# The forget-gate strips of an HGRN branch as seven block products, their weight sums on GpSimd and their snapshots on ScalarE

## The chip, the cores and the metric

The kernel is one program on one core of a Trainium2 chip. The metric is device time in microseconds (us). Everything is float32.

## The reference

A two-layer block feeds a second block. The part that matters is the HGRN branch of the second block's token mix. From 256 latent tokens (taken in column-major order of a 4 x 64 grid, "permuted") and 256 context tokens it computes, for 8 heads of width 128 and in two directions, forget gates and keys from one projection, and then a chunked scan:

```
seg_c = _split_proj(xc @ w_in + b_in)
seg_l = _split_proj(xl @ w_in + b_in)
...
def _hgrn_gates(f_pre, lb):
    fp = f_pre.astype(jnp.float32)
    logf = jnp.log(lb + (1.0 - lb) * jax.nn.sigmoid(fp))
    k = (1.0 - lb) * jax.nn.sigmoid(-fp)
    return logf, k
...
cf, cb, gc = prep(seg_c)
lf, lbw, gl = prep(tuple(_to_col_major(a) for a in seg_l))
hc, hl = _bidir_scan(_hgrn_scan, cf, cb, lf, lbw, init)
```

`f_pre` is what the change is about: 2 directions x 1024 channels, for 256 latent and 256 context tokens each, from 1024 inputs.

## The kernel before

**Layout.** Channels lie on the 128 partitions, tokens along a row. `U` holds the normalized tokens (8 channel tiles, 256 latents and then 256 contexts), `UP` (the memory of `H1`) the latents permuted. Weights come in strips of 256 columns into four slots `W[0]` to `W[3]`. PSUM is eight banks, each handed over by a semaphore `free[b]`. The whole order of work is written out by hand, engine by engine, with counted semaphores between them.

**The recurrence.** The 8 heads are worked in 4 pairs (`i` = 0 to 3). For each pair TensorE projects the query strip (slot 0), one forget strip for each direction (slots 1 and 2) and the value strip (slot 3), and computes the scan as a tree of products: a diagonal product, then levels 0 to 7 (`levels`), context products (`context`), output (`values`) and a mean of squares for the head's norm (the matmul with `mean_c`, here **omean**). On the other engines, level by level, VectorE (`advance`, `pick`) and ScalarE (`lookup`) prepare the operands of the next level.

**The weave.** So that TensorE does not wait for them, the projections of the next pair are Python generators that yield after each matmul, and `weave(steps, n)` issues the next n of them between the levels. I call such a matmul (128 x 128 weights against 256 tokens) a **step**. In pair i the steps are, in this order: value strip of pair i (32), then query strip (16) and forget strips of pair i+1 (32 each, `steps_f`); for the last pair three gate strips (16 each) stand in place of the query and forget strips. `WEAVE` and `WEAVE_LAST` say how many go where; what is left is issued behind omean. The forget strips of pair 0 stand unwoven ahead of the loop (the **opening**), after the query strip.

**A forget strip before** fills two banks, one for each 128 output channels, and in each the 256 latents and the 256 contexts, 8 steps each. When a bank is done ScalarE reads it twice with a sigmoid (`forget`, into `FF_` and `KK`), VectorE scales both (`gates`), and frees the way to `KSUM` (the sum of the keys), which the next pair's diagonal product waits for (`lev_ready`).

**The end of a pair**, in program order: omean; ScalarE turns it into `RS` (a Ln and an Exp); VectorE normalizes and gates the output (`OT`, `HHT`: in the trace L3230 and L3238); the second direction's gates; KSUM. Elsewhere the kernel already uses seven block products in place of eight (`seven_products`), with weight sums on VectorE or half on GpSimd (L1705, L1707), snapshots of PSUM on ScalarE and `assemble` on VectorE.

```
            def token_sums(tokens, o):

                tt(o[0], tokens(0, 1), tokens(0, 0), ALU.subtract).then_inc(S.order_dve, p.inc(S.order_dve))
                eng.wait_ge(S.order_dve, p.now(S.order_dve))
                tt(o[1], tokens(1, 1), o[0], ALU.subtract).then_inc(S.order_dve, p.inc(S.order_dve))
                eng.wait_ge(S.order_dve, p.now(S.order_dve))
                tt(o[2], tokens(1, 1), tokens(0, 1), ALU.subtract)
                tt(o[3], tokens(1, 0), o[1], ALU.subtract).then_inc(S.tsum, p.inc(S.tsum))
```

## Time and profile before

| | |
|---|---|
| time, median of 3 runs | 2031.46 us (2029.79 to 2031.55) |
| the profiled execution's own time | 2030.01 us |
| its span, first to last instruction | 2028.3 us |
| TensorE busy | 1992.8 us (98%) |
| VectorE busy | 1219.1 us (60%) |
| ScalarE busy | 558.7 us (28%) |
| GpSimd busy | 175.7 us (9%) |
| HBM traffic | 270.38 MB read, 134 GB/s over the span |

The busy share is an average over stages. The page cuts the span into 40 slices of 50.7 us; the recurrence lies in slices 29 to 34. PE is TensorE's matmuls, PEld its weight loads, DVE VectorE, ACT ScalarE, POOL GpSimd. A float32 matmul appears as two records, so 16 records are 8 steps.

### The profile page before, as it was taken

The page shows a single profiled execution, that of the slowest core. Times are in us where ns is not written, and L with a number is a line of the kernel's source. Part 1 is how long each engine was busy: PE and PEld are TensorE (multiplying, and loading weights), DVE is VectorE, ACT ScalarE, POOL GpSimd, SP SyncE. Part 2 cuts the span into 40 slices and gives each one's busy share as a digit, 9 for nine tenths or more (in the row PEclk, how much of TensorE's full clock was granted, in tenths as well). Part 3 has the DMA queues.
Part 4 walks back from the last instruction along what each step waited for, and adds up shares of the span by engine and source line. Part 5 has one row for each costly group of instructions (what it writes and reads, how often), then busy time and mean ns, then how long its engine had stood idle before and what let it go on. Part 6 is the DMA issues. An engine that isn't in the chain of part 4 may idle for free.

```text
span 2028.3 us, 31156 instructions
## 1 busy us (share of the span) xinstructions
PE 1992.8 (98%) x12521; PEld 1782.7 (88%) x12521; DVE 1219.1 (60%) x2492; ACT 558.7 (28%) x1342; POOL 175.7 (9%) x232
## 2 busy tenths in 40 slices
PE   9999999999999999999999999999999999999998
PEld 7867999977789999888888878888889889989998
DVE  5424987571278975899769565333344555766664
ACT  3343332223443323111110023222332323232212
POOL 5110341311013300000000001000000000000000
PEclk9999999999999999999999999999999999999999
DMA  6254445442554542555545445332222224545552
GB/s 193 89 166 136 162 162 172 121 144 71 168 166 146 190 144 83 166 166 166 169 156 164 139 122 169 106 96 85 63 79 67 63 63 136 171 131 179 172 175 79
DMA packets 274873, 273.61 MB, mean 135 GB/s; under 512 B 11022, under 2 KB 272378, under 8 KB 274730
## 3 DMA queue, kind: packets, MB, share of 16 engines
q1 hardware_dynamic: 272920, 267.65, 41.4%
q0 software_dynamic: 1216, 3.32, 0.6%
q8 instruction: 100, 1.64, 0.3%
q10 hardware_dynamic: 594, 0.65, 0.1%
q14 instruction: 43, 0.35, 0.1%
HBM read 270.38 MB, written 1.08 MB: 134 GB/s over the span
## 4 chain that ended last, share of the span: by engine, by line
PE 92%; DVE 4%; ACT 1%; DMA 1%; issue 1%; SPq 0%; DVEq 0%; ACTq 0%
PE bank L790 49%; PE bank L1254 11%; PE bank L777 8%; PE bank L1433 5%; PE bank L919 3%; PE bank L1447 2%; PE bank L978 2%; PE bank L1030 1%; PE bank L1498 1%; PE bank L1419 1%; PE bank L1460 1%; DMA W<-in_ada_w_dram 1%; PE bank L989 1%; PE bank L1171 1%; PE bank L1165 1%
## 5 line engine op out<-in xcount | busy, mean ns | idle before, releaser
L790 PE MATMUL bank<-arena,SQ 128*128 128x136 f32 (+2 forms) x2176 | 341.5, 308 | 2.6 <-ACT arena L1793 2.6
L790 PEld LDWEIGHTS bank<-arena,SQ 128*128 128x128 f32 x2176 | 307.0, 191 | 19.8 <-ACT arena L1793 2.8
L790 PE MATMUL bank<-arena,W 128*128 128x136 f32 (+2 forms) x1824 | 272.6, 301 | 2.7 <-issue 2.1
L790 PEld LDWEIGHTS bank<-arena,W 128*128 128x128 f32 x1824 | 247.6, 191 | 15.4 <-issue 4.1
L1793 ACT ACTIVATE H<-bank 128x128 f32<-128x128 f32 (+1 forms) x260 | 82.3, 317 | 537.0 <-PE bank L790 537.0
L790 PE MATMUL bank<-U,W 128*128 128x136 f32 (+2 forms) x1296 | 194.6, 303 | 0.0
L790 PEld LDWEIGHTS bank<-U,W 128*128 128x128 f32 x1296 | 176.4, 191 | 10.9 <-issue 2.9
L777 PE MATMUL bank<-U,W 128*128 128x272 f32 (+2 forms) x608 | 140.6, 392 | 2.4 <-DVEq L2452 1.2
L777 PEld LDWEIGHTS bank<-U,W 128*128 128x128 f32 (+1 forms) x608 | 111.7, 185 | 29.9 <-issue 3.9
L2845 DVE SCALAR_TENSOR_TENSOR W<-W,CC 128x256 f32<-128x256 f32 x280 | 128.3, 483 | 7.0
L790 PE MATMUL bank<-arena 128*128 128x136 f32 (+1 forms) x1024 | 124.1, 278 | 0.0
L790 PEld LDWEIGHTS bank<-arena 128*128 128x128 f32 x1024 | 120.6, 191 | 0.0
L1254 PE MATMUL bank<-W,U 128*128 128x256 f32 (+1 forms) x512 | 100.5, 355 | 0.0
L790 PE MATMUL bank<-U,SQ 128*128 128x136 f32 (+2 forms) x608 | 98.2, 304 | 0.0
L1254 PEld LDWEIGHTS bank<-W,U 128*128 128x128 f32 x512 | 86.8, 190 | 11.5 <-issue 2.0
L1793 ACT ACTIVATE arena<-bank 128x136 f32<-128x136 f32 x176 | 49.1, 279 | 169.9 <-PE bank L790 169.9
L790 PEld LDWEIGHTS bank<-U,SQ 128*128 128x128 f32 x608 | 85.9, 191 | 4.1
L1254 PE MATMUL bank<-arena 128*128 128x256 f32 (+3 forms) x352 | 66.2, 332 | 0.0
L1705 POOL TENSOR_TENSOR SQ<-W 128x512 f32<-128x512 f32 x32 | 40.7, 1272 | 278.9 <-PE bank L790 278.9
L1254 PEld LDWEIGHTS bank<-arena 128*128 128x128 f32 (+2 forms) x352 | 52.2, 179 | 14.1 <-issue 4.0
L2746 DVE SCALAR_TENSOR_TENSOR arena<-arena,PL 128x270 f32<-128x270 f32 x72 | 62.7, 871 | 2.6
L919 PE MATMUL bank<-arena,W 128*128 128x272 f32 x256 | 60.3, 394 | 1.4 <-ACT arena L1783 1.4
(428 smaller groups left out, 3016.2 us busy)
## 6 DMA issues: line engine op xcount, KB each, us to landing
W<-in_ffn_w_up_dram SPq DMA_DIRECT2D x44, 1024.0 KB, 5.1
W<-in_ffn_w_in_dram SPq DMA_DIRECT2D x44, 1024.0 KB, 5.1
W<-in_ada_w_dram SPq DMA_DIRECT2D x36, 1024.0 KB, 7.4
W<-in_mix_w_in_dram SPq DMA_DIRECT2D x36, 1024.0 KB, 5.4
W<-in_w_in_dram SPq DMA_DIRECT2D x22, 1024.0 KB, 5.3
W<-in_ffn_w_down_dram SPq DMA_DIRECT2D x16, 1408.0 KB, 6.5
W<-in_ffn_w_out_dram SPq DMA_DIRECT2D x16, 1408.0 KB, 6.4
W<-in_w_out_dram SPq DMA_DIRECT2D x8, 1024.0 KB, 8.5
```

Of the source, the lines that this page charges most:

```text
L777: last = mm(bank[b][0:m, 0:n], W[r][:, kk, t * P:t * P + m], rhs(kk), start=kk == 0, stop=kk == k - 1)
L790: last = mm(o, a(k), b[:, k], start=not adds and k == 0, stop=k == kt - 1, skip_group_check=True)
L919: return mm(bank[2 * (r % 2) + t][:, c0:c0 + n], W[r][:, k, t * P:(t + 1) * P], rhs(k), start=k == 0, stop=k == KD - 1, skip_group_check=True)
L978: last = mm(o, U[:, kk, t0:t0 + w], W[r][:, kk, 0:SW], start=kk == 0, stop=kk == KD - 1)
L989: last = mm(bank[b][:, 0:T1], W[r][:, kk, t * P:(t + 1) * P], u1(kk), start=kk == 0, stop=kk == KD - 1)
L1254: last = mm(o, x, y, start=i == 0, stop=i == n - 1 and bias is None, skip_group_check=True)
L1433: last = mm(bank[b][:, c:c + SEQ], W[r][:, k, t * P:(t + 1) * P], src[:, k, c:c + SEQ], start=k == 0, stop=k == KD - 1, skip_group_check=True)
L1447: last = mm(bank[b][:, c:c + SW], tok(k), W[r][:, k, :], start=k == 0, stop=k == KD - 1, skip_group_check=True)
L1705: eng.tensor_tensor(WS[n % 2][:, 0], part(1, 0), part(1, 1), ALU.add).then_inc(S.order_pool, p.inc(S.order_pool))
L1793: act(sn[:, i, :], bank[b][:, c:c + w], ACT.Copy).then_inc(S.snap, p.inc(S.snap))
L2746: stt(CZ[:, i, 2:], Z[:, g % 2, i, 0:T1 - 2], w(0), CZ[:, i, 2:], ALU.mult, ALU.add).then_inc(sem, p.inc(sem))
L2845: ins = stt(o, x, c, o, ALU.mult, ALU.add) if k else ts(o, x, c, None, ALU.mult)
```

## The change

Each forget strip is cut into four blocks of weights (two halves of the inputs by two tiles of the outputs) and four blocks of tokens (two halves of the inputs by the two token groups: permuted latents and contexts). Seven products of 4 steps replace eight. They need four sums of token blocks, once (`token_sums` into `TBR`, on VectorE after the second pair of the memory stage that comes before), and four sums of weight blocks for each strip (GpSimd, into `WSR`: a new loop at the end of its program). The partial results are copied out of PSUM as they stand by ScalarE (`kept`, four copies for each strip into `SNR`) and added up on VectorE (`fold`, three additions), which frees the banks; ScalarE's two sigmoids then read the folded result from SBUF. `WSR` shares its memory with `TBU`, so the latents' token sums for the merge move from before the recurrence to its last pair. The numbers of the weave change (pre 14, ctx 12). Two semaphores of the convolution norm become one (no instruction changes). The diff without these declarations:

```
@@ -51,8 +51,8 @@
-WEAVE = dict(pre=10, diag=6, lev=8, ctx=10, av=10, om=12)
-WEAVE_LAST = dict(pre=8, diag=4, lev=6, ctx=8, av=6, om=6)
+WEAVE = dict(pre=14, diag=6, lev=8, ctx=12, av=10)
+WEAVE_LAST = dict(pre=8, diag=4, lev=6, ctx=8, av=6)
@@ -422,6 +423,9 @@
+        SN_LATE = cut(2, SEQ)
+        TBR = [H2[:, 0:4, SEQ:2 * SEQ], H2[:, 4:8, SEQ:2 * SEQ], cut(4, SEQ), cut(4, SEQ)]
+        SNR = [[W[2 * d][:, SK - 1, :], W[2 * d + 1][:, SK - 1, :], SN_LATE[:, 0, :], SN_LATE[:, 1, :]] for d in range(2)]
@@ -461,6 +465,10 @@
+        def permuted_and_context(h, c):
...
+            return (UP[:, 4 * h:4 * h + 4, 0:SEQ], U[:, 4 * h:4 * h + 4, SEQ:2 * SEQ])[c]
@@ -1422,20 +1430,56 @@
-            def steps_f(r):
+            def steps_f(r, first=False):
...
+                bx = 2 * (r % 2)
+                by = bx + 1
+                near, far = slice(0, SEQ), slice(SEQ, 2 * SEQ)
...
+                def raw(t, h, k):
+                    return W[r][:, 4 * h + k, t * P:(t + 1) * P]
...
+                def add(o, x, y, k, clear, ends=True):
+                    ins = mm(o, x, y, start=clear and k == 0, stop=k == 3, skip_group_check=True)
+                    if ends and k == 3:
+                        ins.then_inc(S.prod, p.inc(S.prod))
+                    return ins
                 eng.wait_ge(S.land[r], p.next(S.land[r], 16))
-                for t in range(2):
-                    b = 2 * (r % 2) + t
-                    take(b)
-                    for c, src in ((0, UP), (SEQ, U)):
-                        for k in range(KD):
-                            last = mm(bank[b][:, c:c + SEQ], W[r][:, k, t * P:(t + 1) * P], src[:, k, c:c + SEQ],
-                                      start=k == 0, stop=k == KD - 1, skip_group_check=True)
-                            if c and k == KD - 1:
-                                sem = S.done[r] if t else S.half[r]
-                                last.then_inc(sem, p.inc(sem))
-                            yield
+                take(bx)
+                for k in range(4):
+                    add(bank[bx][:, near], raw(0, 0, k), permuted_and_context(0, 0)[:, k], k, True)
+                    yield
+                take(by)
+                for k in range(4):
+                    add(bank[by][:, near], raw(0, 1, k), permuted_and_context(1, 0)[:, k], k, True, False)
+                    yield
+                if first:
+                    eng.wait_ge(S.tsum, p.next(S.tsum))
+                eng.wait_ge(S.wsum, p.next(S.wsum))
+                eng.wait_ge(S.snap, p.next(S.snap))
+                for k in range(4):
+                    add(bank[bx][:, far], WSR[0][:, k], TBR[0][:, k], k, False)
+                    yield
+                for k in range(4):
+                    add(bank[by][:, far], raw(1, 1, k), TBR[3][:, k], k, True)
+                    yield
+                eng.wait_ge(S.wsum, p.next(S.wsum))
+                eng.wait_ge(S.snap, p.next(S.snap))
+                for k in range(4):
+                    add(bank[bx][:, near], WSR[1][:, k], TBR[1][:, k], k, False)
+                    yield
+                eng.wait_ge(S.wsum, p.next(S.wsum))
+                eng.wait_ge(S.snap, p.next(S.snap, 2))
+                for k in range(4):
+                    add(bank[bx][:, far], WSR[3][:, k], permuted_and_context(1, 1)[:, k], k, False)
+                    yield
+                eng.wait_ge(S.wsum, p.next(S.wsum))
+                for k in range(4):
+                    ins = add(bank[bx][:, near], WSR[2][:, k], TBR[2][:, k], k, False)
+                    if k == 0:
+                        ins.then_inc(S.done[r], p.inc(S.done[r]))
+                    yield
@@ -1525,9 +1569,10 @@
             p.leave("recurrence")
+            places["sums"] = (p.now(S.prod), p.now(S.wsum))
             weave(steps_q(0), None)
             columns()
-            for steps in (steps_f(1), steps_f(2)):
+            for steps in (steps_f(1, True), steps_f(2)):
                 weave(steps, None)
@@ -1734,6 +1779,21 @@
+            p.meet("recurrence")
+            prod, wsum = places["sums"]
+            p.skip(S.prod, prod - p.now(S.prod))
+            p.skip(S.wsum, wsum)
+            for n in range(2 * PAIRS):
+                r = 1 + n % 2
+                part = lambda t, h: W[r][:, 4 * h:4 * h + 4, t * P:(t + 1) * P]
+                eng.wait_ge(S.land[r], p.next(S.land[r], 16))
+                for o, x, y, op, used in ((0, part(1, 0), part(1, 1), ALU.add, 2), (1, WSR[0], part(0, 0), ALU.subtract, 2),
+                                          (3, part(0, 1), WSR[1], ALU.subtract, 1), (2, part(0, 0), part(1, 0), ALU.subtract, 1)):
+                    if n:
+                        eng.wait_ge(S.prod, p.next(S.prod, used))
+                    eng.tensor_tensor(WSR[o], x, y, op).then_inc(S.wsum, p.inc(S.wsum))
+                    eng.wait_ge(S.wsum, p.now(S.wsum))
@@ -2235,17 +2296,26 @@
+            def kept(d, which):
...
+                bx = 2 * ((1 + d) % 2)
+                x, z, y = bank[bx][:, 0:SEQ], bank[bx][:, SEQ:2 * SEQ], bank[bx + 1][:, SEQ:2 * SEQ]
+                for n in which:
+                    eng.wait_ge(S.prod, p.next(S.prod))
+                    i, src = ((0, x), (3, z), (2, y), (1, x))[n]
+                    act(SNR[d][i], src, ACT.Copy).then_inc(S.snap, p.inc(S.snap))
+                    if n == 3:
+                        p.skip(S.prod, 2)
+                        p.skip(S.done[1 + d])
...
             def forget(i, d, t):
-                r = 1 + d
-                b = 2 * (r % 2) + t
-                sem = S.done[r] if t else S.half[r]
-                eng.wait_ge(sem, p.next(sem))
-                act(FF_[i % 2][:, d, t, :], bank[b][:, :], ACT.Sigmoid, bias=col(B_HF + 8 * d + t, i * 2))
-                act(KK[i % 2][:, :, d, t, :], bank[b][:, :].rearrange("p (a b) -> p a b", a=2), ACT.Sigmoid, scale=-1.0,
-                    bias=NB[:, i * 2 + 8 * d + t:i * 2 + 8 * d + t + 1]).then_inc(S.fk, p.inc(S.fk))
+                F = FF_[i % 2][:, d, t, :]
+                eng.wait_ge(S.f_raw, p.next(S.f_raw))
+                act(KK[i % 2][:, :, d, t, :], F.rearrange("p (a b) -> p a b", a=2), ACT.Sigmoid, scale=-1.0,
+                    bias=NB[:, i * 2 + 8 * d + t:i * 2 + 8 * d + t + 1])
+                act(F, F, ACT.Sigmoid, bias=col(B_HF + 8 * d + t, i * 2)).then_inc(S.fk, p.inc(S.fk))
                 eng.wait_ge(S.fk, p.now(S.fk))
-                eng.sem_inc(S.free[b], 1)
@@ -2278,6 +2348,7 @@
             for d in range(2):
+                kept(d, range(4))
                 for t in range(2):
@@ -2293,8 +2364,10 @@
                         query(i + 1, lev - 5)
+                    if more and lev == 5:
+                        kept(0, (0,))
                 if more:
-                    forget(i + 1, 0, 0)
+                    kept(0, (1, 2, 3))
                 else:
@@ -2304,7 +2377,8 @@
                 if more:
-                    forget(i + 1, 0, 1)
+                    kept(1, (0,))
+                    forget(i + 1, 0, 0)
                 else:
@@ -2314,11 +2388,12 @@
                 eng.sem_inc(S.free[7], 1)
+                if more:
+                    forget(i + 1, 0, 1)
+                    kept(1, (1, 2, 3))
                 eng.wait_ge(S.o_full, p.next(S.o_full))
                 act(OSQ, bank[6][:, :], ACT.Square).then_inc(S.osq, p.inc(S.osq))
-                if more:
-                    forget(i + 1, 1, 0)
-                else:
+                if not more:
                     next(early)
@@ -2327,7 +2402,8 @@
                 if more:
-                    forget(i + 1, 1, 1)
+                    for t in range(2):
+                        forget(i + 1, 1, t)
                 else:
@@ -3112,6 +3189,24 @@
                     arguments(i + 1)
+                if i == 1:
+                    token_sums(permuted_and_context, TBR)
...
+            def fold(i, d):
...
+                bx = 2 * ((1 + d) % 2)
+                by = bx + 1
+                F = FF_[i % 2][:, d]
+                eng.wait_ge(S.snap, p.next(S.snap, 4))
+                tt(F[:, 0, 0:SEQ], SNR[d][0], bank[by][:, 0:SEQ], ALU.add).then_inc(S.order_dve, p.inc(S.order_dve))
+                eng.wait_ge(S.order_dve, p.now(S.order_dve))
+                eng.sem_inc(S.free[by], 1)
+                eng.wait_ge(S.prod, p.next(S.prod, 6))
+                tt(F[:, 0, SEQ:2 * SEQ], SNR[d][1], bank[bx][:, SEQ:2 * SEQ], ALU.add).then_inc(S.f_raw, p.inc(S.f_raw))
+                tt(F[:, 1, :].rearrange("p (a b) -> p a b", a=2), SN_LATE, bank[bx][:, 0:SEQ].unsqueeze(1).to_broadcast([P, 2, SEQ]),
+                   ALU.add).then_inc(S.f_raw, p.inc(S.f_raw))
+                eng.wait_ge(S.f_raw, p.now(S.f_raw))
+                eng.sem_inc(S.free[bx], 1)
@@ -3191,10 +3286,11 @@
             p.meet("recurrence")
-            token_sums(latent_tokens, TBU)
+            p.skip(S.wsum, 4 * 2 * PAIRS)
             eng.wait_ge(S.hib, p.next(S.hib, 16))
...
             for d in range(2):
+                fold(0, d)
                 for t in range(2):
@@ -3218,10 +3314,11 @@
                 if more:
+                    fold(i + 1, 0)
                     gates(i + 1, 0, 0)
                     gates(i + 1, 0, 1)
-                    gates(i + 1, 1, 0)
                 else:
+                    token_sums(latent_tokens, TBU)
                     p.meet("merge")
@@ -3238,6 +3335,8 @@
                 if more:
+                    fold(i + 1, 1)
+                    gates(i + 1, 1, 0)
                     gates(i + 1, 1, 1)
```

TensorE, the end of pair 0 up to the first woven steps behind the second pair's diagonal product (L1433 and L1443 are steps of a forget strip, L1447 and L1491 of the value strip, L1476 and L1520 the diagonal product, L1544 and L1589 omean). Before:

```order
L1433 MATMUL bank<-H,W 128x256 [waits free1]
L1433 MATMUL bank<-H,W 128x256 x3
L1544 MATMUL bank<-arena,mean_c 128x512 [waits free7,osq]
L1433 MATMUL bank<-H,W 128x256 x4
L1433 MATMUL bank<-U,W 128x256 x8
L1447 MATMUL bank<-W,H 128x256 [waits free2,land3]
L1447 MATMUL bank<-W,H 128x256 x9
L1476 MATMUL bank<-arena 128x128 [waits free4,lev_ready]
```

Now:

```order
L1443 MATMUL bank<-U,W 128x256 [waits snap,wsum]
L1443 MATMUL bank<-U,W 128x256 x3
L1443 MATMUL bank<-arena,W 128x256 [waits wsum]
L1443 MATMUL bank<-arena,W 128x256 x3
L1589 MATMUL bank<-arena,mean_c 128x512 [waits free7,osq]
L1491 MATMUL bank<-W,H 128x256 [waits free2,land3]
L1491 MATMUL bank<-W,H 128x256 x13
L1520 MATMUL bank<-arena 128x128 [waits free4,lev_ready]
```

Between omean and the diagonal product there were 12 + 10 steps and are now 14; ahead of the last pair 12 + 8 become 8. All of the forget strips' steps now lie ahead of omean.

VectorE at the same place (L3230/L3327 and L3238/L3335 are OT and HHT, L3121/L3122 and L3216/L3217 the gates, L3201 to L3206 `fold`, L3203/L3299 KSUM). Before:

```order
L3121 TENSOR_SCALAR arena<-arena,LBC 128x512 [waits fk,order_dve]
L3122 TENSOR_SCALAR arena<-arena,LBC 128x2x256
L3230 SCALAR_TENSOR_TENSOR arena<-bank,P,RS 128x256 [waits ors,order_dve]
L3230 SCALAR_TENSOR_TENSOR arena<-bank,P,RS 128x256
L3238 TENSOR_TENSOR SQ<-arena 128x64x4 [waits order_dve]
L3238 TENSOR_TENSOR SQ<-arena 128x64x4
L3121 TENSOR_SCALAR arena<-arena,LBC 128x512 [waits fk]
L3122 TENSOR_SCALAR arena<-arena,LBC 128x2x256
L3203 TENSOR_TENSOR arena<-arena 128x512 [waits order_dve,hq]
```

Now:

```order
L3335 TENSOR_TENSOR SQ<-arena 128x64x4 [waits order_dve]
L3335 TENSOR_TENSOR SQ<-arena 128x64x4
L3201 TENSOR_TENSOR arena<-W,bank 128x256 [waits snap]
L3205 TENSOR_TENSOR arena<-W,bank 128x256 [waits order_dve,prod]
L3206 TENSOR_TENSOR arena<-arena,bank 128x512
L3216 TENSOR_SCALAR arena<-arena,LBC 128x512 [waits f_raw,fk]
L3217 TENSOR_SCALAR arena<-arena,LBC 128x2x256
L3216 TENSOR_SCALAR arena<-arena,LBC 128x512 [waits fk,order_dve]
L3217 TENSOR_SCALAR arena<-arena,LBC 128x2x256
L3299 TENSOR_TENSOR arena<-arena 128x512 [waits order_dve,hq]
```

Before, one pair of gate instructions stood between HHT and KSUM; now the second direction's fold and all of its gates stand there.

ScalarE in level 5 of a pair (L2323 is the lookup, L2295 the query's Silu, L2306 a snapshot), now:

```order
L2295 ACT_TABLE_LOAD
L2295 ACTIVATE arena<-bank,P 128x256 [waits half0]
L2306 ACTIVATE W<-bank 128x256 [waits hq,prod]
L2323 ACTIVATE arena<-arena 128x512 [waits ks,lev_full]
L2295 ACTIVATE arena<-bank,P 128x256 [waits done0]
L2306 ACTIVATE arena<-bank 128x256 [waits hq,prod]
```

The first snapshot of the next pair's first forget strip stands behind a table load and a Silu.

## Rows read from the trace of the kernel before

**Rows 1.** The page: TensorE's busy row, its granted clock by slices, the chain.

```profile
PE 1992.8 (98%) x12521; PEld 1782.7 (88%) x12521; DVE 1219.1 (60%) x2492; ACT 558.7 (28%) x1342; POOL 175.7 (9%) x232
...
PEclk9999999999999999999999999999999999999999
...
PE 92%; DVE 4%; ACT 1%; DMA 1%; issue 1%; SPq 0%; DVEq 0%; ACTq 0%
```

**Rows 2.** The forget strips' line: duration of a record, count, first and last start.

```profile
L1433 PE MATMUL bank<-H,W x256: 379/379/382, 1424.7 to 1642.6; 128*128 128x256 f32 x128
L1433 PE MATMUL bank<-U,W x256: 379/379/382, 1428.2 to 1646.1; 128*128 128x256 f32 x128
```

**Rows 3.** Timeline of TensorE at pair 2's end: after omean, and the last pair's diagonal.

```profile
1641.11 1.89 PE L1433 MATMUL bank<-H,W 128*128 128x256 f32 x8
...
1649.74 1.07 PE L1476 MATMUL bank<-arena 128*128 128x128 f32 x8
```

**Rows 4.** Timeline (start, duration) of pair 1's end, from omean's end on.

```profile
1576.46 1.89 PE L1433 MATMUL bank<-H,W 128*128 128x256 f32 x8
...
1578.27 0.88 DVE L3230 SCALAR_TENSOR_TENSOR arena<-bank,P,RS 128x256 f32<-128x256 f32 x2 [1.88 <-ACT RS L2328]
1579.29 1.06 DVE L3238 TENSOR_TENSOR SQ<-arena 128x256 f32<-128x256 f32 x2
...
1581.64 4.48 PE L1447 MATMUL bank<-W,H 128*128 128x256 f32 x20
...
1581.84 0.69 ACT L2244 ACTIVATE arena<-bank,P 128x512 f32<-128x512 f32 x1 [2.37 <-PE bank L1433]
1582.42 0.68 ACT L2245 ACTIVATE arena<-bank,NB 128x512 f32<-128x512 f32 x1
...
1584.25 0.69 DVE L3203 TENSOR_TENSOR arena<-arena 128x512 f32<-128x512 f32 x1 [0.17 <-DVE arena L3122]
...
1585.96 1.05 PE L1476 MATMUL bank<-arena 128*128 128x128 f32 x8
```

**Rows 5.** VectorE additions with one PSUM operand elsewhere, grouped: busy us, mean ns.

```profile
L2605 DVE TENSOR_TENSOR arena<-H,bank 128x512 f32<-128x512 f32 x14 | 9.6, 687 | 3.2 <-PE bank L790 2.2
...
L2595 DVE TENSOR_TENSOR arena<-H,bank 128x256 f32<-128x256 f32 x14 | 5.9, 421 | 2.3 <-ACT H L1793 0.5
```

**Rows 6.** Timeline of pair 1's level 4 on TensorE and ScalarE.

```profile
1542.87 0.63 ACT L2253 ACTIVATE arena<-arena 128x512 f32<-128x512 f32 x1 [2.60 <-DVE arena L3151]
...
1543.52 1.28 ACT L2234 ACT_TABLE_LOAD   x1
1543.57 3.62 PE L1433 MATMUL bank<-H,W 128*128 128x256 f32 x16
...
1544.82 0.47 ACT L2234 ACTIVATE arena<-bank,P 128x256 f32<-128x256 f32 x1
```

**Rows 7.** Timeline of the opening: first forget strip, the queries, the first value strip.

```profile
1424.72 3.62 PE L1433 MATMUL bank<-H,W 128*128 128x256 f32 x16
...
1427.90 1.07 ACT L2234 ACTIVATE arena<-bank,P 128x256 f32<-128x256 f32 x2
...
1452.35 4.48 PE L1447 MATMUL bank<-W,H 128*128 128x256 f32 x20
```

**Rows 8.** GpSimd's weight sums in layer one, and VectorE's convolution beside them (min/median/max ns).

```profile
L1705 POOL TENSOR_TENSOR SQ<-W x32: 1265/1272/1279, 214.1 to 699.5; 128x512 f32<-128x512 f32 x32
...
L2746 DVE SCALAR_TENSOR_TENSOR arena<-arena,PL x72: 499/501/1395, 215.8 to 714.5; 128x270 f32<-128x270 f32 x72
```

**Rows 9.** VectorE's waits in the memory stage, third pair (timeline; in brackets the idle before).

```profile
1329.84 0.42 DVE L3030 TENSOR_TENSOR arena<-bank,arena 128x256 f32<-128x256 f32 x1 [3.54 <-PE bank L1254]
...
1344.10 1.29 DVE L3041 TENSOR_TENSOR arena<-bank,arena 128x512 f32<-128x512 f32 x2 [12.92 <-PE bank L1254]
```

**Rows 10.** Timeline: TensorE's first matmuls of the program, and same-sized pairs late in it.

```profile
2.84 4.61 PE L727 MATMUL bank<-ident 128*128 128x128 f32 x20 [2.84 <-POOL LNT L1615]
...
1697.52 1.95 PE L790 MATMUL bank<-U,W 128*128 128x128 f32 x16
```

21 lines of the change are left out of this document (12 added, 9 removed).

## The prediction

> **What bounds the kernel now.** I read the page first: TensorE is busy 98% of the span at full clock in every slice, and the chain that ended last is 92% TensorE [rows 1]. So a removed matmul is worth its full time, as long as nothing else comes to the front. The next view is the forget strips' own line: 512 records, two for a matmul, so 256 steps, all between 1424.7 and 1646.1 us [rows 2]. A step's price is best read start to start: from omean's end at 1641.11 to the last pair's diagonal product at 1649.74 stand 12 + 8 = 20 steps, 8.63 us, so 0.432 us each [rows 3]. The same sum for pair 1, 12 + 10 steps, is 1585.96 - 1576.46 = 9.50 us [rows 4]: TensorE never stands still there.
>
> The third view is the timeline of the other engines at that place, because TensorE is full there only thanks to its 22 (20) steps. Let T be the start of the first step behind omean. VectorE, released by ScalarE's RS, starts OT at T+1.81 and ends HHT at T+3.89 (1580.35). The last forget step ends at T+5.18 (1581.64), two sigmoids run to 1583.10, the gates to KSUM's start at 1584.25, KSUM ends at 1584.94, T+8.48 [rows 4]. For pairs 0 and 1 that is 1.0 us before TensorE wants it, at the last pair 0.15 us [rows 3]. This cover is what the change spends.
>
> **The change part by part.** *Removed:* 4 of 32 steps for each of 8 strips, 32 x 0.432 = **-13.8 us** if TensorE stays busy.
>
> *End of a pair.* The steps between T and the diagonal product fall to 14 for pairs 0 and 1 and to 8 for pair 2. TensorE arrives at T+6.04 and T+3.45. The chain that it then waits for is one sequence, nothing in it side by side: HHT ends at T+3.9; the fold's first addition 0.42 (a 128x256 addition with a PSUM operand), about 0.17 for the wait on it (the gap in front of KSUM in rows 4), the second 0.42: T+4.85, where the first sigmoid pair can start, since the third addition (0.69) goes on beside it [rows 4, 5]. A sigmoid pair took 1.26 (1581.84 to 1583.10). There are now two behind each other, as both tiles of the direction wait for this fold: T+4.9 to T+6.15 and, with 0.1 between dependent instructions, T+6.25 to T+7.5. The second tile's gates and the wait behind them take 1.15, KSUM 0.69: T+9.35, and the product starts some 0.1 later [rows 4]. I take **T+9.5**. That is where it starts today (9.50), and 0.87 later than today at the last pair (8.63). So at pairs 0 and 1 the 8 saved steps come back whole as a wait of 3.46 us each; at pair 2 the wait is 6.05 us.
>
> *Snapshots.* A copy of 128x256 out of PSUM costs about 0.47 and starts 0.2 after the step that made it [rows 4, 6]. Two of the four gate TensorE closely. The fourth copies a block that the 20th step finished, and the 21st waits for it: 0.2 + 0.47 + 0.13 = 0.8 us with nothing between when a strip stands unwoven. In the woven first strip a level stands there, in the second the output products, so it costs nothing. The first copy must be there at the 9th step. In level 4 TensorE reaches that at 1543.57 + 4 x 0.432 = 1545.30; ScalarE by then has a lookup, a table load and the query's Silu in its program first, to 1545.29, and the copy ends near 1545.9 [rows 6]: **0.7 us** in each of three pairs, 2.1 us. In the second strip the copy has the whole of level 7 and the context products ahead of it and is free.
>
> *The opening.* The first strip would run from 1424.72; its 9th step is due at 1428.17, but the queries hold ScalarE to 1428.97 and the copy to about 1429.5: 1.5 us. Fourth copy 0.8. In the second strip the first copy stands behind the first fold and two sigmoid pairs (3.4 us after the first strip's end, plus 0.5), due after 3.45: 0.55, and again 0.8. Together 3.65 against 8 saved steps, 3.45: the second strip ends at 1452.5 instead of 1452.35 [rows 7]. Behind it come 14 steps and not 10, +1.73. The chain of fold, sigmoids, gates and KSUM needs 5.1 us there and is covered by 6.04.
>
> *From a diagonal product to the next T* both versions issue 90 steps (6+64+10+10 before, 6+64+12+8 now), so beyond the 0.7 nothing changes.
>
> *Weight sums on GpSimd.* 8 x 4 instructions at 1.27 us [rows 8]. They form one buffer, but each sum is due 24 steps (10.4 us) after the product that frees its place, and the first strip's weights are there 30 us early: no wait. They can hold up VectorE: beside such sums an instruction of 0.50 us took up to 1.39 [rows 8]. By the rows one meeting costs up to 0.9 us. VectorE is busy 60% of the span [rows 1] and so has room between levels that TensorE paces, and the sums freed by the last steps of a strip end near T+0.6, before OT. I take 0. The Trainium skill ("SBUF — State Buffer", "SBUF: two separate sides") says that the loser of the shared port waits for the whole instruction of the other; that speaks against putting 41 us of GpSimd work here, and 9 meetings on the path would by it make +8 us of my 0.
>
> *Token sums.* Four additions of 1024, some 5 us by the 0.69 for 512 [rows 5], at the end of the memory stage's second pair, where VectorE waits 3.5 us and then, after three short instructions, 12.9 us for TensorE [rows 9]. Hidden; uncovered they would cost 1.5 us. The latents' sums move to an idle stretch of the last pair, 0. Strips' slots come free after 25 steps of 28, so the loads are no later.
>
> *Sum:* opening +0.2, 4 more steps behind it +1.7, level 4 +2.1, last pair +0.9: **+4.9 us**. Counted the other way: -13.8 + 3.65 + 2.1 + 3.46 + 3.46 + 6.05 = +4.9.
>
> **The clock.** TensorE has no gap in the recurrence now, and its granted clock never falls after the start [rows 1]. But its very first matmuls, after 2.84 us of nothing, took 4.61 us for 20 records of 128x128, 0.23 each, where 16 such records late in the program take 1.79 start to start, 0.11 each [rows 10]: half speed, at a cost of up to 2.4 us. The new waits are longer than that first gap. I expect half clock (1.2 GHz) after the 6.05 us one, and not after the two of 3.46. Between 0 and 2.4 I take 1.6, since in the first level the other engines' chain hides a part. The Trainium skill ("TensorE: Matmul & The Clock Gate", "Why this matters for your kernels") warns of gaps in TensorE's work for the same reason; if every gap is paid, that is the third rival below.
>
> So +6.5 us: the profiled execution would go from 2030.0 to 2036.5, the median, 1.45 above it, from 2031.5 to **2038.0 us**.
>
> **The rivals.** A difference under 0.2% (4.1 us) can't be told from none.
> 1. *Forecast*: the chain of fold and sigmoids ends each pair, the clock falls once. 2038; 0.38.
> 2. *Same chain, clock holds*: 2031.5 + 4.9 = 2036.4; 0.27. For it: no gap inside a running stage has been seen to cost clock. Against: the start.
> 3. *All three gaps cost the full 2.4*: 2031.5 + 4.9 + 7.2 = 2043.6; 0.10. Against: two gaps are only a little longer than the start's.
> 4. *GpSimd's sums stretch the chain*: nine meetings of 0.9, on top of 4.9, 2044.5; 0.06. Against: their places above.
> 5. *The cover is enough (faster)*: let L be the chain from T to the diagonal product. The sum is -13.8 + 3.65 + 2.1 + 2(L - 6.04) + (L - 3.45) = 3L - 23.6. It turns at L = 7.9, and beats 0.2% below 6.5. At L = 6.04, where pairs 0 and 1 fit under 14 steps, it gives 2026; 0.07. For it: the number 14 fits such a chain. Against: L would have to be less than HHT's end plus two sigmoid pairs, gates and KSUM (8.4).
> 6. *In between*: L near 8.7 and half of the snapshot waits hidden, 2031.5 + 1.5 = 2033; 0.12.
>
> **How the numbers follow.** Range 2033.0 to 2043.0: it leaves out most of cases 3, 4 and 5. Case 1 alone spans 2036 to 2040. Slower by over 0.2% (above 2035.5): 0.38 + 0.10 + 0.06 + two thirds of case 2 = 0.71. Within: the rest of case 2 and case 6, 0.22. Faster: 0.07.
>
> **What would show it.** In the changed profile: 448 records on the forget strips' line; TensorE idle before the diagonal products of pairs 1 to 3 by 3.5, 3.5 and 6 us, released by VectorE's KSUM; from T to these products 9.5 us; 0.7 us of idle in level 4 released by ScalarE; in the opening four waits of 0.5 to 1.5 us; a lower clock digit near the last pair. I am wrong if the waits at the diagonal products are under 1 us, or if VectorE's instructions in the levels are longer than now and TensorE waits at the levels.

## The result and the profile after

The changed kernel took **2041.16 us** (median of 4 runs, 2040.54 to 2043.95) where the kernel before, on the same chip, took 2031.51 us (2029.79 to 2031.79). The ratio is 1.0049, 95% interval 1.0036 to 1.0061: slower by 9.65 us, beyond the 0.2% that can be told from none. It lies inside the predicted range, 3.2 us above the predicted 2038.0. The profiled execution took 2040.54 us, its span is 2038.4 us.

The rows of the page that answer to [rows 1]; the third is the chain that ended last, by engine:

```profile
PE 1986.1 (97%) x12457; PEld 1773.7 (87%) x12457; DVE 1239.8 (61%) x2520; ACT 572.0 (28%) x1374; POOL 216.8 (11%) x264
...
PEclk9999999999999999999999999999999999999999
...
PE 90%; DVE 5%; ACT 3%; issue 1%; DMA 1%; DVEq 0%; POOL 0%; SPq 0%; ACTq 0%; POOLq 0%
```

TensorE has 64 records fewer (32 steps) and is busy 6.7 us less, yet the span is 10.1 us longer. The clock row can't say why: a slice is 51 us, and a few microseconds at half clock vanish in it. The forget strips' line now has 256 + 128 + 64 = 448 records, as the change says:

```profile
L1443 PE MATMUL bank<-H,W x256: 379/379/455, 1425.3 to 1639.8; 128*128 128x256 f32 x128
L1443 PE MATMUL bank<-arena,W x128: 379/379/382, 1432.2 to 1646.7; 128*128 128x256 f32 x128
L1443 PE MATMUL bank<-U,W x64: 379/379/454, 1436.4 to 1645.0; 128*128 128x256 f32 x64
```

TensorE's waits in the recurrence (line waited for: us in total, times, longest) are two, and before there was none:

```profile
PE bank L1520 <- DVE arena L3299: 12.0, 3, 5.7
PE bank L1443 <- ACT W L2306: 4.3, 7, 1.5
```

L1520 is the diagonal product, L3299 KSUM; L2306 is ScalarE's snapshot. The end of pair 1 in the timeline (start, duration; in brackets the idle time before), which answers to [rows 4]:

```profile
1580.73 6.21 PE L1491 MATMUL bank<-W,H 128*128 128x256 f32 x28
...
1582.47 0.88 DVE L3327 SCALAR_TENSOR_TENSOR arena<-bank,P,RS 128x256 f32<-128x256 f32 x2 [10.72 <-ACT RS L2403]
1583.49 1.06 DVE L3335 TENSOR_TENSOR SQ<-arena 128x256 f32<-128x256 f32 x2
1584.39 0.41 DVE L3201 TENSOR_TENSOR arena<-W,bank 128x256 f32<-128x256 f32 x1
1584.95 0.42 DVE L3205 TENSOR_TENSOR arena<-W,bank 128x256 f32<-128x256 f32 x1
...
1585.40 0.72 ACT L2315 ACTIVATE arena<-arena,NB 128x512 f32<-128x512 f32 x1 [1.74 <-DVE arena L3205]
1586.03 0.70 ACT L2317 ACTIVATE arena<-arena,P 128x512 f32<-128x512 f32 x1
1586.77 0.72 ACT L2315 ACTIVATE arena<-arena,NB 128x512 f32<-128x512 f32 x1
...
1587.40 0.71 ACT L2317 ACTIVATE arena<-arena,P 128x512 f32<-128x512 f32 x1
...
1589.34 0.69 DVE L3299 TENSOR_TENSOR arena<-arena 128x512 f32<-128x512 f32 x1 [0.18 <-DVE arena L3217]
...
1590.08 1.16 PE L1520 MATMUL bank<-arena 128*128 128x128 f32 x8 [3.15 <-DVE arena L3299]
1591.08 1.55 PE L1491 MATMUL bank<-W,H 128*128 128x256 f32 x4
1592.42 3.10 PE L1491 MATMUL bank<-W,U 128*128 128x256 f32 x8
```

T is 1580.73. HHT ends at T+3.82, the first sigmoid starts at T+4.67, and the fourth ends at T+7.38; KSUM ends at T+9.30, and the product starts at T+9.35. It is one sequence, with TensorE idle for the last third. The two rows behind the product show something else: 4 records in 1.55 us and 8 in 3.10, where such groups take 1.03 and 1.89 at full clock.

The granted clock is read in short windows (bounds, length, each engine's busy time, then the clock, DMA share and rate), one behind each diagonal product:

```profile
1526.00:1531.00 5.00, 5.00 (x27) 4.56 (x26) 2.62 (x7) 1.19 (x2) 0.00 (x0) 1.00 0.00 0
...
1591.00:1595.40 4.40, 4.40 (x16) 3.58 (x15) 1.66 (x5) 1.28 (x2) 0.00 (x0) 0.61 0.01 2
...
1657.00:1662.00 5.00, 4.86 (x16) 4.23 (x17) 2.71 (x7) 1.52 (x3) 0.00 (x0) 0.50 0.00 0
```

Behind pair 0's wait of 3.15 us the clock is full, behind pair 1's equal one it is 0.61, mostly half clock (1.2 GHz), and behind the last one, 5.73 us, it is 0.50. From the product to the level products behind it everything is slowed, and the other engines' chain hides little of it.

**The ledger.** I take the length of the recurrence from the first forget strip to the merge's first projection: 1697.52 - 1424.72 = 272.80 us before, 1707.74 - 1425.35 = 282.39 us after, so +9.59. (Of the rest, 0.63 lies ahead of it, and what follows is 0.12 shorter.) By places: opening +0.41, steps behind it +1.73, from product to product +0.63 (over pair 0's end), +0.72 (pair 1's) and +3.28 (pair 2's), from the last product to the merge +2.82. The half clock behind pair 1's wait lies in the third of these stretches: without its 1.7 us the third would be +1.6.

### The profile page after: what moved, and what is told of

Same layout as the page of the kernel before. It is cut to its first block, busy times and chain, and to the rows that moved or that the text cites. A ratio compares the mean times of both kernels' runs of the same rounds, so it can differ in the third digit from the quotient of the medians.

```text
span 2038.4 us, 31190 instructions
## 1 busy us (share of the span) xinstructions
PE 1986.1 (97%) x12457; PEld 1773.7 (87%) x12457; DVE 1239.8 (61%) x2520; ACT 572.0 (28%) x1374; POOL 216.8 (11%) x264
## 4 chain that ended last, share of the span: by engine, by line
PE 90%; DVE 5%; ACT 3%; issue 1%; DMA 1%; DVEq 0%; POOL 0%; SPq 0%; ACTq 0%; POOLq 0%
PE bank L798 51%; PE bank L1262 11%; PE bank L785 8%; PE bank L1443 4%; PE bank L927 3%; PE bank L986 2%; PE bank L1491 2%; PE bank L1038 1%; PE bank L1542 1%; PE bank L1504 1%; DMA W<-in_ada_w_dram 1%; PE bank L997 1%; PE bank L1173 1%; PE bank L1179 1%; PE bank L1059 0%
## 5 line engine op out<-in xcount | busy, mean ns | idle before, releaser
L798 PEld LDWEIGHTS bank<-U,W 128*128 128x128 f32 x1296 | 176.4, 191 | 10.9 <-issue 2.9
L1794 POOL TENSOR_TENSOR W<-W 128x512 f32<-128x512 f32 x32 | 40.7, 1271 | 288.1 <-PE bank L1443 188.4
```

Source lines behind the costliest of these rows:

```text
L798: last = mm(o, a(k), b[:, k], start=not adds and k == 0, stop=k == kt - 1, skip_group_check=True)
L1794: eng.tensor_tensor(WSR[o], x, y, op).then_inc(S.wsum, p.inc(S.wsum))
```

## The experiments

Each row gives the median, the ratio to the kernel before on the same chip with its 95% interval, the profiled recurrence by the measure above, and TensorE's waits at the three diagonal products.

| run | median us | ratio | recurrence us | waits us |
|---|---|---|---|---|
| the change | 2041.16 | 1.0049 (1.0036 to 1.0061) | 282.39 | 3.15, 3.15, 5.73 |
| b0_changed_again | 2043.77 | 1.0063 (1.0048 to 1.0078) | 282.11 | 3.15, 3.15, 5.73 |
| a1_busy | 2046.18 | 1.0072 (1.0056 to 1.0089) | 286.60 | none |
| b2_busy_half | 2037.14 | 1.0033 (1.0019 to 1.0047) | 277.96 | 0.47, 0.47, 0.38 |
| c2_busy_last | 2043.25 | 1.0049 (1.0032 to 1.0066) | 283.63 | 3.25, 3.25, 0.39 |
| a2_numbers | 2036.82 | 1.0027 (1.0017 to 1.0038) | 277.89 | 0.72, 0.72, 3.15 |
| a3_hoist | 2027.01 | 0.9978 (0.9968 to 0.9987) | 266.36 | 0, 0, 0.86 |
| a4_snap_first | 2037.88 | 1.0029 (1.0016 to 1.0041) | 276.20 | 3.15, 3.15, 5.73 |
| a5_double_sums | 2045.92 | 1.0076 (1.0061 to 1.0091) | 282.13 | 3.16, 3.15, 5.73 |
| c1_double_again | 2042.49 | 1.0055 (1.0039 to 1.0072) | 286.28 | 3.15, 3.15, 5.73 |
| b1_all | 2021.75 | 0.9956 (0.9941 to 0.9971) | 260.75 | none |
| c3_hoist_snap | 2021.02 | 0.9945 (0.9930 to 0.9960) | 261.93 | 0, 0, 0.86 |

### Is what follows the waits the clock's?

Matmuls that nobody needs are put ahead of the diagonal product's wait, in a bank that this product overwrites:

```
-            def levels(par, steps, w):
+            def levels(par, steps, w, fill=0):
...
-                eng.wait_ge(S.lev_ready, p.next(S.lev_ready))
                 take(4)
+                keep_busy(bank[4][:, 0:P], fill)
+                eng.wait_ge(S.lev_ready, p.next(S.lev_ready))
...
-                levels(i % 2, steps, w)
+                levels(i % 2, steps, w, (0, 24, 24, 48)[i])
```

**a1_busy**, expected:

> The changed kernel, with 24, 24 and 48 idle-filling matmuls of 128x128 (0.112 us each, so 2.7 and 5.4 us) issued ahead of the wait for the diagonal product of the second, third and last pair; nothing else. Theory (the chain of fold and sigmoids sets the length, and the clock falls in the gaps, 1.7 us behind the third pair's and 2.8 us behind the last pair's in the profile): the three products still start at T+9.35, the clock stays at full speed, 2041.2 - 4.5 = 2036.7 us (2035.5 to 2038). Rival (the time behind these products is lost to something else, GpSimd or the levels): unchanged, 2041.

It took 2046.2 us. I had mis-sized the filler: each such matmul is two records, so 24 of them took 5.52 us and 48 took 10.88:

```profile
1590.55 5.52 PE L772 MATMUL bank<-mean_d,ident 128*128 128x128 f32 x48
```

The filler outlasted the waits and made the products late. Against the next run, from product to product, that is 2.05, 1.95 and 4.71 us, and 277.96 + 8.7 = 286.7 where the recurrence measures 286.60. The levels behind it ran at full clock. That fits but is no clean test, so it was repeated with half the counts, (0, 12, 12, 24).

**b2_busy_half**, expected:

> The kernel of a1_busy with half as many extra matmuls ahead of the diagonal product (12, 12 and 24, at two records of 0.112 us each: 2.7, 2.7 and 5.4 us, all inside the waits of 3.15, 3.15 and 5.73 us). Theory: the 4.5 us that the changed kernel loses after its waits is the clock's alone, so it comes back and the chain's end stays where it was: 2041.2 - 4.5 = 2036.7 us (up to 2038 if the short gap that is left lets the clock fall once), all products at full speed. Rival: the loss after the waits isn't the clock's (the levels wait for something else there): 2041 us.

It took 2037.1 us. The last pair, after a filler of 5.52 us:

```profile
1655.96 1.16 PE L1521 MATMUL bank<-arena 128*128 128x128 f32 x8 [0.38 <-DVE arena L3300]
1656.95 1.89 PE L1491 MATMUL bank<-W,H 128*128 128x256 f32 x8
```

8 records in 1.89 us, not 3.62 as in the changed kernel. Work that nobody needs made the recurrence 4.43 us shorter than the change's. In the medians it is 4.0 us against the change's first measurement and 6.6 us against b0_changed_again on the same chip. The chain's end stayed where it was (the product starts at T+9.35), so what follows the waits is the clock's.

**c2_busy_last** fills only the last wait, (0, 0, 0, 24); expected:

> The extra matmuls only in the last pair (24, 5.4 us, in the wait of 5.73 us), none in the two waits of 3.15 us. Theory: the last gap's fall of the clock (2.8 us) comes back for certain, and one of the two shorter gaps still falls in most executions (1.7 us): 2041.2 - 2.8 = 2038.4 us, and 1.3 to 1.7 us above b2_busy_half (2037.1), with one of the two pairs showing matmuls at half speed behind its wait. Rival: with the last gap filled neither short one falls, 2037 us; or the short gaps are what sets the last one, 2041 us.

It took 2043.25 us, 4.85 above the expectation. The last pair is as in b2_busy_half (47.85 us from its product to the merge, 47.87 there). But in the profiled execution both shorter gaps lost clock, and the diagonal product itself ran at half speed:

```profile
1526.51 2.04 PE L1521 MATMUL bank<-arena 128*128 128x128 f32 x8 [3.25 <-DVE arena L3300]
...
1594.71 2.05 PE L1521 MATMUL bank<-arena 128*128 128x128 f32 x8 [3.25 <-DVE arena L3300]
```

From one product to the next it is 68.20 and 68.13 us, against 65.38 in b2_busy_half: 2.8 us for each. So the half of the expectation that a short gap falls once, for 1.7 us, is refuted. Its recurrence also started 1.2 us later than b2_busy_half's (1427.06 against 1425.87).

**b0_changed_again**, the changed kernel unaltered; expected:

> The changed kernel once more, unchanged, beside the runs that follow. 2041.2 us as before. For the clock: in the first profile pair 1's wait of 3.15 us was followed by half-speed matmuls (1.7 us lost) and pair 0's equal wait was not. If the length of the gap alone decided it, both would fall or both would hold; if it is decided by something that varies from one execution to the next (say by where the gap lies against a period of the chip's own), this profile can show another pattern: the last gap of 5.73 us falls again in either case.

It took 2043.8 us. Here pair 0 lost the clock and pair 1, which had lost it in the first profile, did not:

```profile
1528.74 1.20 PE L1520 MATMUL bank<-arena 128*128 128x128 f32 x8 [3.15 <-DVE arena L3299]
1529.74 1.92 PE L1491 MATMUL bank<-W,H 128*128 128x256 f32 x4
1531.44 2.73 PE L1491 MATMUL bank<-W,U 128*128 128x256 f32 x8
...
1595.81 1.16 PE L1520 MATMUL bank<-arena 128*128 128x128 f32 x8 [3.15 <-DVE arena L3299]
1596.80 1.03 PE L1491 MATMUL bank<-W,H 128*128 128x256 f32 x4
```

The gaps' lengths are the same to 0.01 us, so length alone does not decide. This profiled execution took 3.7 us more than the first, and none of it is in the recurrence (282.11 against 282.39): the first forget strip starts at 1429.40, not 1425.35.

### Is GpSimd's work free?

**a5_double_sums** adds one more GpSimd subtraction behind each weight sum; expected:

> The changed kernel with one more GpSimd subtraction (128x384, on a buffer that nothing of this stage reads) behind each of the 24 weight sums. Theory: GpSimd's work in the recurrence costs nothing in the changed kernel, since it runs beside VectorE operations that nobody waits for: 2041.2 us, same. Rival 4 of the prediction: GpSimd's sums stretch the chain at a pair's end. Then doubling that work costs again what it cost once: the two-input operations of the chain (HHT 1.06, the sums and gates) are up to 1.1 us longer each where they meet, up to 3 x 1.0 to 3 x 2.5 us: 2044 to 2049 us, and the chain's end behind T moves from T+9.35 to T+10.4 or more.

```
                     eng.wait_ge(S.wsum, p.now(S.wsum))
+                    eng.tensor_tensor(mask01[:, :], mask01[:, :], mask01[:, :], ALU.subtract).then_inc(S.order_pool, p.inc(S.order_pool))
+                    eng.wait_ge(S.order_pool, p.now(S.order_pool))
```

(There are 32 sums, and so 32 additions, not 24 as I wrote.) The median was 2045.9 us, 2.2 above b0_changed_again beside it, which by itself speaks for the rival. The trace does not: the waits are the same, and so is the chain's beginning beside the added work.

```profile
1586.18 0.83 POOL L1796 TENSOR_TENSOR mask<-mask 128x384 f32<-128x384 f32 x1
1586.60 0.88 DVE L3329 SCALAR_TENSOR_TENSOR arena<-bank,P,RS 128x256 f32<-128x256 f32 x2 [10.15 <-ACT RS L2405]
1587.62 1.06 DVE L3337 TENSOR_TENSOR SQ<-arena 128x256 f32<-128x256 f32 x2
...
1594.22 1.16 PE L1520 MATMUL bank<-arena 128*128 128x128 f32 x8 [3.15 <-DVE arena L3301]
```

T is 1584.86 and the product starts at T+9.36, as without the extra work. HHT keeps its 1.06 us per pair of instructions, but the added subtraction had ended ahead of it, so this run is no test of what a meeting with HHT costs. It left 2.2 us of medians with no place, and the same kernel was run again.

**c1_double_again**, expected:

> a5_double_sums once more. Its median was 2045.9 us against 2043.8 and 2041.2 us of the changed kernel, but its profiled execution (2042.7 us, span 2040.6) shows the recurrence as long as the changed kernel's (282.1 us from the first strip to the merge, against 282.1 and 282.4) and the same waits of 3.16, 3.15 and 5.73 us. Theory: the rest isn't the sums' but the clock's, which falls in more or fewer places from one execution to the next, and a second set lies where the changed kernel's do, 2040.4 to 2044.3 us. Rival: GpSimd's extra work does lengthen something outside the chain, and the median stays at 2045 to 2046 us, with a place that shows it.

The median was 2042.5 us (2040.72 to 2048.27), and the profiled execution was the slowest one. It shows where such a time comes from: both short gaps fell fully.

```profile
1528.57 2.07 PE L1520 MATMUL bank<-arena 128*128 128x128 f32 x8 [3.15 <-DVE arena L3301]
...
1596.72 2.08 PE L1520 MATMUL bank<-arena 128*128 128x128 f32 x8 [3.15 <-DVE arena L3301]
```

Its recurrence is 286.28 us: b2_busy_half's 277.96 plus three falls, 2.8 us each, is 286.4. It also began 3.9 us later than in the change's first profile. One execution of the same kernel took 2040.7 us, so the doubled sums need not cost anything. The mean granted clock on record for each execution points the same way: at 0.993 the doubled kernel took 2043.99 us and the change 2043.67 to 2044.28; at 0.995 and 0.996 the doubled one took 2040.72 to 2042.72 and the change 2040.43 to 2041.19. The doubled kernel's slowest three (2047 to 2048 us) have 0.991 and 0.992. So rival 4, a longer chain, falls; why these executions had more half clock is not shown.

### The weave's numbers, and the order of the chain

**a2_numbers**, with `WEAVE = dict(pre=16, diag=6, lev=7, ctx=12, av=8)`; expected:

> The changed kernel with other weave numbers for the first three pairs (pre 16, level 7 in place of 14 and 8): 6 forget steps are left behind omean, so 22 steps stand between T and the diagonal product of the second and third pair and 14 before the last. Theory: the chain keeps its length of 9.35 us, two waits of 3.15 us vanish, the last falls from 5.7 to 3.3 us, and most of the clock's 4.5 us comes back: 2041.2 - 6.3 - 2.4 - 4.5 = 2028 us, up to 2030 if the clock still falls once. Rival (the levels have no slack for a step less each, or GpSimd's sums lengthen VectorE's work there): waits of some 0.4 us come up at 24 levels, 2033 or more.

It took 2036.8 us: of the 13.2 us expected, 4.4 came. The waits at the product became 0.72, 0.72 and 3.15 us, because the chain had grown to T+10.4: one of GpSimd's sums now lay beside HHT.

```profile
1582.95 2.08 DVE L3335 TENSOR_TENSOR SQ<-arena 128x256 f32<-128x256 f32 x2
1583.08 1.48 POOL L1794 TENSOR_TENSOR W<-W 128x512 f32<-128x512 f32 x1 [0.46 <-PE bank L1443]
```

And the strips came to stand against the snapshots at new places:

```profile
PE bank L1443 <- ACT W L2306: 7.8, 13, 1.5
```

The clock still fell once, behind the last wait of 3.15 us. So both the theory (the gaps shrink) and the rival (new waits) had a part.

**a3_hoist** puts the second direction's fold, sigmoids, gates and KSUM ahead of the norm's Ln and Exp and of OT and HHT, on both engines. On ScalarE:

```
-                if not more:
-                    next(early)
+                if more:
+                    for t in range(2):
+                        forget(i + 1, 1, t)
+                else:
+                    next(early)
                 tables(LOG_EXP)
```

and on VectorE OT and HHT become a function `finish(i)`, called behind the gates. Expected:

> The changed kernel, with the second direction's fold, sigmoids and gates ahead of the norm's Ln and Exp on ScalarE and ahead of OT and HHT on VectorE, which move behind the next pair's KSUM and query products. Theory: the chain no longer starts at HHT but at the last forget step, and the diagonal product is ready near T+5: no wait at the second and third pair, 1.5 us at the last, no fall of the clock: 2041.2 - 6.3 - 4.3 - 4.5 = 2026 us. Rival (the norm's chain is needed as early as before, or bank 6 and 7 are freed too late): the waits move to the levels, 2035 or more.

It took 2027.0 us. Pair 1's end:

```profile
1579.44 0.42 DVE L3205 TENSOR_TENSOR arena<-W,bank 128x256 f32<-128x256 f32 x1 [5.99 <-PE bank L1443]
...
1580.10 6.21 PE L1491 MATMUL bank<-W,H 128*128 128x256 f32 x28
...
1583.83 0.69 DVE L3315 TENSOR_TENSOR arena<-arena 128x512 f32<-128x512 f32 x1 [0.18 <-DVE arena L3217]
...
1586.14 1.05 PE L1520 MATMUL bank<-arena 128*128 128x128 f32 x8
```

The fold starts ahead of T, KSUM ends at T+4.42, and TensorE goes through its 14 steps into the product at T+6.04 with no wait. The output's chain (OT at 1585.64, T+5.54, where it was T+1.74) is 3.8 us later and nobody waits for it. The recurrence is 16.0 us shorter than the change's: 11.2 of waits and 4.5 of clock. This settles what the end-of-pair wait was: the order on the two engines, not the amount of their work.

**a4_snap_first** puts the first snapshot of a strip ahead of what ScalarE had in its program there (the table load and the Silu; in the opening the queries' work, and one pair of sigmoids). In the levels:

```
+                    if more and lev == 5:
+                        kept(0, (0,))
                     if more and lev > 4:
                         query(i + 1, lev - 5)
-                    if more and lev == 5:
-                        kept(0, (0,))
```

> The changed kernel, with each strip's first snapshot ahead of the query's Silu (in level 5 and in the opening) and ahead of the second sigmoid pair in the opening; nothing else. Theory: three waits of 0.5 to 0.6 us in level 4 and two of 1.5 and 0.3 us in the opening vanish: 2041.2 - 3.4 = 2037.8 us. Rival (these waits only stand in for later ones at the same place): unchanged within 1 us.

It took 2037.9 us. The wait on snapshots fell to

```profile
PE bank L1443 <- ACT W L2306: 1.1, 2, 0.6
```

and the waits at the products stayed. From the product behind pair 0's wait to the one behind pair 1's it is 64.66 us, 0.71 less than the change's 65.37, for a wait that the profile puts at 0.48. The recurrence of 276.20 is 6.2 us shorter than the change's: 1.7 are pair 1's fall of the clock, which did not come here in either short gap, and 4.5 are the snapshots. The same edit on top of a3_hoist (c3_hoist_snap, below) gives 4.4.

### A version that beats both

**b1_all**, both edits and `WEAVE_LAST = dict(pre=14, diag=4, lev=6, ctx=6, av=4)`; expected:

> Both edits that gained, together: the second direction's work ahead of the norm's (a3_hoist, 2027.0 us) and the first snapshot ahead of the Silus (a4_snap_first, -3.3 us), and in the last pair, which has no chain behind it that anybody waits for in the levels, the vector work spread as far as the pre steps reach (pre 14, ctx 6, av 4). Theory: the snapshot waits and the chain's waits are separate costs, so they add: 2027.0 - 3.3 - up to 1 = 2022.7 to 2023.7 us, waits on W's snapshot about 1 us in all. Rival: the snapshot ahead of the Silus delays ScalarE's sigmoids, which the hoisted chain needs, so that the gain of one is given back: 2026 to 2027 us.

It took 2021.75 us, **0.9956 (0.9941 to 0.9971)** of the kernel before. **c3_hoist_snap**, without these numbers; expected:

> b1_all without its last-pair numbers: the second direction's work ahead of the norm's, and the first snapshot ahead of the Silus. Theory: the last pair's wait of 0.86 us is all that the numbers took away in b1_all: 2021.75 + 0.9 = 2022.7 us (2022 to 2024). Rival: the last-pair numbers also saved or cost steps elsewhere: 2021 or 2025 us.

It took 2021.02 us, **0.9945 (0.9930 to 0.9960)**. The last pair's wait of 0.86 us is there, as expected, and the recurrence is 1.2 us longer than b1_all's, but the medians do not show it. I keep the simpler kernel, c3_hoist_snap: 10.9 us less recurrence than before, of the 13.8 that 32 steps are worth. Of the missing 2.9 the profile shows 2.2: 1.1 us of waits on snapshots and 0.9 and 0.2 us on VectorE in the last pair.

## Why the prediction was right

**The step's price and the count**: right. 448 records, and TensorE's removed work came back as waits. The eight steps of a pair were saved and lost again at its end.

**End of a pair**: right. T+9.5 was forecast and T+9.36, T+9.35 and T+9.34 measured; waits of 3.46, 3.46 and 6.05 were forecast and 3.15, 3.15 and 5.73 measured. Part of that difference is the 0.14 us, the rest that an idle time starts where the last matmul's modelled end is. The second fold addition ended at T+4.64, where I had said 4.85 (my own terms, 3.89 + 0.42 + 0.17 + 0.42, add up to 4.90), and a pair of sigmoids took 1.33 (1585.40 to 1586.73) instead of 1.26.

**Snapshots**: right in the sum. A copy took 0.38 us, not the 0.47 that I took from the next row. The opening's four waits were 1.48, 0.57, 0.30 and 0.56, where 1.5, 0.8, 0.55 and 0.8 were forecast, yet the opening grew by 0.41 us against +0.2: the profile's idle times are less than what a stop costs from start to start (in pair 1's level 4 it was 0.48 of idle and, by a4_snap_first, 0.71 of time, where I had 0.7).

**The sum without the clock** has a direct measurement, b2_busy_half's recurrence: 277.96 - 272.80 = **+5.2 us**, where +4.9 was forecast. By places, up to the last product, it was 0.39 + 1.73 + 0.63 + 0.72 + 1.60 = 5.07; forecast were 0.2 + 1.7 + 0.7 + 0.7 + 1.6.

**The clock** is the term that was mis-sized. I expected one fall, 1.6 us. The first profile has 4.5: 2.8 at the last pair and 1.7 at pair 1. The reason for taking 1.6 and not 2.4, "since in the first level the other engines' chain hides a part", was wrong: the fall behind the gap of 5.73 us cost 2.8 us against the kernel before (2.7 against b2_busy_half), and almost nothing hid it. The reason for sparing the two gaps of 3.46 us was that they are only a little longer than the start's 2.84 us of nothing, which sets no threshold for a clock that was already full. How many gaps fall is luck of the execution: the change's two profiles have two falls each, at different pairs, a4_snap_first's has one and c1_double_again's three. The truth lay between the forecast and rival 3. With 4.5 in place of 1.6 the forecast would have been 2030.0 + 1.45 + 4.9 + 4.5 = 2040.9, beside the measured 2041.2. That sum leaves no term of GpSimd's.

One premise was a misreading. That "its granted clock never falls after the start" was read from slices of 51 us, and with it stands rival 2's "no gap inside a running stage has been seen to cost clock". In the kernel before, ahead of the memory stage, TensorE waits 0.59 and then 1.80 us, and the granted clock of the 5 us around its next matmuls is 0.66. The changed kernel's first profile has the same waits and kept its clock there, so the same two matmuls took 1.10 us. Before, and then the changed kernel:

```profile
1206.12 2.05 PE L757 MATMUL bank<-SQ,mean_d 128*128 128x512 f32 x2 [1.80 <-DVE tick L2947]
1205.00:1210.00 5.00, 3.88 (x15) 2.87 (x16) 1.64 (x5) 2.62 (x5) 0.00 (x0) 0.66 0.56 145
...
1206.84 1.10 PE L765 MATMUL bank<-SQ,mean_d 128*128 128x512 f32 x2 [1.81 <-DVE tick L3024]
```

A table of short stretches over the old profile would have shown one fall behind a stop shorter than the new ones and, in the first layer, none behind a stop of 2.61 us: a matter of odds, where I took a length as the bound.

**GpSimd** at 0 was right for this order of work and is not safe. The meeting that rival 4 feared came in a2_numbers, and took 1.0 us of the chain in each of the first two pairs. Doubling the sums where the change has them cost nothing on the chain. That the Trainium skill ("SBUF — State Buffer", "SBUF: two separate sides") gives the shared port to one of the two for a whole instruction agrees with HHT's 1.06 us becoming 2.08 beside a sum; here the price came where the chain's two-input instructions met one, and only there.

**Token sums**: right, hidden. No wait for them is in the recurrence. The 0.6 us ahead of it are no evidence by themselves, as the first forget strip starts between 1425.35 and 1429.40 over the profiles of kernels that are alike up to there. But the stretch that holds the sums has a length too: from the matmuls at 1202.50 (1203.21 in the changed kernel) to the first forget strip it is 222.22 us before and 222.14 now, and 222.24 in b1_all, whose clock falls at the same place as before. Uncovered they were to cost 1.5 us.

**Rival 5** needed L below 7.9. The change had L = 9.35, and a3_hoist, which has L = 6.04 at pairs 0 and 1 by another order, took 2027.0, where the rival's formula gives 2026 (its last wait was 0.86, not 2.6, as the hoisted chain is shorter than that: KSUM ends at T+4.4). With 0.86 the same sum gives 2024, and the recurrence, 6.4 us shorter than before, 2025; the rest up to the median has no place.

**The chances.** The terms given for "slower" add up to 0.72 and those for "within" to 0.21, not 0.71 and 0.22.

## What to carry to other kernels

When matmuls are removed that stood between the last input of a chain and its consumer, read the chain on the other engines from that point, instruction by instruction: removed cover comes back as a wait of the same length, and here all 16 saved steps of pairs 0 and 1 did. Then look what stands ahead of the chain in the program of each engine; moving work that nobody waits for behind it turned +9.7 us into -4.7, and with the snapshots into -11.7. And cost a new gap in TensorE's work twice: as the gap, and as the half-clock matmuls that may follow it, with a chance read from the gaps that the old profile already has, looked at in short stretches.

## What the runs showed of the hardware

- **The clock after a gap of 3.15 to 3.25 us is not settled by its length.** Of the 13 such gaps in the profiles (two each of the change, b0_changed_again, a5_double_sums, c1_double_again, c2_busy_last and a4_snap_first, one of a2_numbers) five were followed by half clock at once, product included (2.8 us lost each in c1_double_again and c2_busy_last, 1.6 in a2_numbers), three by half clock from 1.0 to 1.4 us after the product's start (1.7 us lost), five by none. One kernel, that with doubled sums, showed all three. All five gaps of 5.73 us fell (2.5 to 2.7 us lost each, by the stretch from the product to the merge against b2_busy_half's); in the recurrence none of 0.38 to 0.86 did. What decides is open; the runs differ in when the gap comes, but no rule was tested.
- **Shorter gaps can cost the clock too.** Outside the recurrence every one of the 13 profiles, the kernel before included, has the same two stops. Behind a wait of 2.61 us in the first layer nine fell and four did not; behind the 0.59 and 1.80 us ahead of the memory stage seven fell and six did not. Before (full clock) and the changed kernel (half) at the first:

```profile
643.47 1.19 PE L790 MATMUL bank<-arena,SQ 128*128 128x136 f32 x8 [2.61 <-ACT arena L1793]
...
642.66 2.18 PE L798 MATMUL bank<-arena,SQ 128*128 128x136 f32 x8 [2.61 <-ACT arena L1853]
```

- **Two profiles of one kernel can differ by 4 us outside the place under study.** The recurrence starts 4.05 us later in b0_changed_again than in the change's first profile. 2.84 us of that are there at the same matmuls of the stage ahead (1206.05 against 1203.21), the rest comes over the next 20 us, where the granted clock was 0.83 against 1.00. For effects of this size the length of the stage was the better measure: with the falls counted it gave 4.5 and 4.4 us for the snapshots, where the medians, each less the kernel before on its own chip, gave 3.5 and 7.0.
- **One of GpSimd's sums beside a two-input VectorE instruction** took it from 1.06 to 2.08 us (two instructions), and itself went from 1.27 to 1.48 us (a2_numbers).
- Not tried on the chip: an order of the products in which TensorE would not wait for the snapshots at all. ScalarE would then read a bank while TensorE writes the other half of it.
